# A centred pooling moved from the tensor engine to the vector engine, and one panel computed channel by channel, in a two-block transformer kernel

## The reference, cut to what matters

```python
POOL_GROUPS, POOL_GROUP_DIM = 4, 512
POOL_WINDOWS = (2, 4, 8, 16)

def centred_multiscale_pool(u):
    """u (B, L, G, Cg): group g averages over a centred window POOL_WINDOWS[g]
    (valid positions only), via prefix sums, minus the token itself."""
    ...
    left = win // 2
    right = win - 1 - left
    hi = jnp.minimum(t + right + 1, L)
    lo = jnp.maximum(t - left, 0)
    s = cs[:, hi, g] - cs[:, lo, g]
    mean = s / (hi - lo)
    return mean - uf

def pool_branch(h, w_in, w_grp, b_grp, scale, w_out):
    u, gate = jnp.split(h @ w_in, 2, axis=-1)
    p = centred_multiscale_pool(u.reshape(B, L, POOL_GROUPS, POOL_GROUP_DIM))
    p = jnp.einsum('blgc,gcd->blgd', p, w_grp) + b_grp
    y = p.reshape(B, L, POOL_WIDTH) * scale
    return (y * jax.nn.silu(gate)) @ w_out

# around it, for the latent and for the context sequence:
shift, scale, gate = jnp.split(jax.nn.silu(c) @ ada_w[i] + ada_b[i], 3, axis=-1)
h = rms_norm(x, pre_norm[i]) * (1 + scale) + shift
x = x + gate * rms_norm(pool_branch(h, ...), post_norm[i])
```

## Time and profile before

| | before |
|---|---|
| median of 3 runs | 2297.24 us |
| profiled execution: time | 2297.67 us |
| profiled execution: span, first to last instruction | 2295.9 us |
| mean granted clock of the tensor engine | 0.998 |
| tensor engine busy | 2269.0 us (99%) |
| vector engine busy | 1678.0 us (73%) |
| ScalarE busy | 1028.4 us (45%) |
| moved by DMA | 430.33 MB |

### The profile page before, as it was taken

The page is one execution under the profiler, slowest core; times in us unless marked ns, Lnnn a source line. Parts: engine busy times, 40 slices in busy tenths (PEclk is TensorE's granted clock), DMA queues, the critical chain, the costliest instruction groups (busy, mean ns, idle before and its releaser), DMA issues.

```text
span 2295.9 us, 30903 instructions
## 1 busy us (share of the span) xinstructions
PE 2269.0 (99%) x11041; PEld 1885.9 (82%) x11041; DVE 1678.0 (73%) x2399; ACT 1028.4 (45%) x1474; POOL 81.5 (4%) x115
## 2 busy tenths in 40 slices
PE   8999999999999999999999999999999999999998
PEld 6878888888888888788888888888888799999986
DVE  5479976688788887666659676766785788788864
ACT  5575655565555555443452222222322544543433
POOL 1023200000000000000000000000000100000000
PEclk9999999999999999999999999999999999999999
DMA  8966645676777676676746555555565367633344
GB/s 244 218 179 209 189 146 165 189 239 210 220 220 232 215 229 219 227 242 214 233 146 203 171 174 160 174 171 167 208 200 158 105 189 222 186 107 112 112 147 147
DMA packets 226233, 430.33 MB, mean 187 GB/s; under 512 B 13879, under 2 KB 38703, under 8 KB 225232
## 3 DMA queue, kind: packets, MB, share of 16 engines
q1 hardware_dynamic: 222400, 418.96, 58.9%
q10 hardware_dynamic: 3152, 9.83, 1.3%
q0 software_dynamic: 576, 0.14, 0.0%
HBM read 426.16 MB, written 2.72 MB: 187 GB/s over the span
## 4 chain that ended last, share of the span: by engine, by line
PE 90%; DVE 3%; DMA 2%; issue 2%; ACT 2%; DVEq 0%; SPq 0%; POOL 0%; ACTq 0%; POOLq 0%
PE ps L644 53%; PE ps L679 13%; PE ps L656 10%; PE ps L2661 2%; PE ps L2636 2%; PE ps L2697 1%; DMA raw<-in_w_up 1%; DVE lo L582 1%; PE ps L2675 1%; PE ps L2526 1%; DVE ustage L1838 1%; PE ps L693 1%; PE ps L2423 1%; PE ps L2689 1%; ACT ustage L1399 1%
## 5 line engine op out<-in xcount | busy, mean ns | idle before, releaser
L578 ACT ACTIVATE hi<-raw 128x1024 fp32r<-128x1024 f32 x604 | 634.4, 1060 | 921.6 <-PE ps L644 424.9
L582 DVE TENSOR_TENSOR lo<-raw,hi 128x1024 fp32r<-128x1024 f32 x604 | 730.9, 1223 | 414.4 <-ACT hi L578 411.7
L613 DVE SCALAR_TENSOR_TENSOR ada_acc<-raw,csil,ada_acc 128x512 f32<-128x512 f32 x660 | 452.3, 750 | 6.6 <-DMA raw<-in_ada_w 6.6
L644 PE MATMUL ps<-hi,h_hi 128*128 128x512 f32 x960 | 382.1, 398 | 0.5 <-DVE lo L582 0.2
L644 PE MATMUL ps<-hi,h_lo 128*128 128x512 f32 x960 | 378.8, 395 | 0.0
L644 PE MATMUL ps<-lo,h_hi 128*128 128x512 f32 x960 | 378.7, 395 | 0.0
L644 PE MATMUL ps<-hi,g 128*128 128x512 f32 x704 | 224.9, 398 | 2.4 <-DVE lo L582 2.4
L644 PEld LDWEIGHTS ps<-hi,h_hi 128*128 128x128 f32 x960 | 180.8, 188 | 44.3 <-DVE lo L582 3.7
L644 PEld LDWEIGHTS ps<-hi,h_lo 128*128 128x128 f32 x960 | 180.8, 188 | 42.4
L644 PEld LDWEIGHTS ps<-lo,h_hi 128*128 128x128 f32 x960 | 180.9, 188 | 40.6
L644 PEld LDWEIGHTS ps<-hi,g 128*128 128x128 f32 x704 | 133.3, 189 | 33.5 <-DVE lo L582 2.9
(11 more groups left out here) (334 smaller groups left out, 3469.8 us busy)
## 6 DMA issues: line engine op xcount, KB each, us to landing
raw<-in_ada_w SPq DMA_DIRECT2D x176, 512.0 KB, 4.2
raw<-in_w_up SPq DMA_DIRECT2D x176, 512.0 KB, 4.5
raw<-in_w_down SPq DMA_DIRECT2D x88, 512.0 KB, 4.8
raw<-in_w_in SPq DMA_DIRECT2D x84, 512.0 KB, 4.6
raw<-in_pool_w_in SPq DMA_DIRECT2D x64, 512.0 KB, 4.5
raw<-in_mla_w_in SPq DMA_DIRECT2D x56, 448.0 KB, 3.9
raw<-in_w_out SPq DMA_DIRECT2D x32, 512.0 KB, 3.7
raw<-in_pool_w_out SPq DMA_DIRECT2D x32, 512.0 KB, 4.4
```

The lines of the kernel that those rows point to most:

```text
L578: act.activation(hi[:, to, :, :], raw[:, slot, :, :], ACT.Copy).then_inc(hi_split, 1 + ada)
L582: dve.tensor_tensor(lo[:, to, :, :], raw[:, slot, :, :], hi[:, to, :, :].bitcast(F32), ALU.subtract).then_inc(lo_split, 1)
L613: ins = dve.scalar_tensor_tensor(acc, raw[:, slot, k, :], csil[:, v, kt:kt + 1], acc, ALU.mult, ALU.add)
L644: mm = pe.matmul(ps[:, bank, 0:n], tokens(a, kt0 + k, tok), w[:, slot, k, col0:col0 + n], start=first and k == 0 and s == 0, stop=last and ...
```

## The change

1. `u` is made channel by channel (`by_channels` in place of `by_tokens`), so it comes out as channels by tokens, the form in which it is needed. The halves of the first panel become matmuls of 256 columns, twice as many.
2. ACT copies it, in two halves of two channel tiles, into `upad`, which has zeros on both sides of each sequence (set once by GpSimd).
3. The pooling matrix and its 32 matmuls a group go. The vector engine sums shifted rows instead: window 2 is one addition, 4, 8 and 16 are two, three and four, each on the sum before it, for either half. One small multiplication corrects the ends of the sequences (`edges`), and one instruction scales the sum and subtracts the token (`scalar_tensor_tensor`, in place in `upad`). These stand amid the splitting of w10 to w13.
4. The group's own matrix moves from w12 and w13 to w14 and w15. The instruction that adds bias and scale moves from DVE to ACT; the bias is multiplied by the scale once, ahead of the stage.
5. The banks change: `u` in banks 0, 1, 6, 7 for group 0 and 0 to 3 for the others, the gate in 2 to 5 and then 4 to 7. The group's second modulation panel, which was turned before w17, is turned in the next group's first panel, between w1 and w2, into two of the gate's banks. For this the tensor engine waits on `gate_silu4` at the start of a group (two of the four silus of the group before) and again before that turn.
6. The panel before w16 (the first of the group) is turned before w17 now.

```diff
+        def window_sums(e, n, half):
+            step = sums_done(n, half) - n - 2
+            spans = [(0, SEQ)]
+            for level in range(n, 0, -1):
+                spans.insert(0, (spans[0][0] - 2 ** (level - 1), spans[0][1] + 2 ** (level - 1)))
+            src = upad[:, 2 * half:2 * half + 2, :, :].rearrange("p m s t -> p (m s) t")
+            buffers = windows[half][0], windows_first2[n] if half == 0 else windows[1][1]
+            for level, (a, b) in enumerate(spans):
+                to = buffers[level % 2]
+                back, ahead = (1, 0) if level == 0 else (2 ** (level - 1), 2 ** (level - 1))
+                if level:
+                    e.wait_ge(window_summed, step + level)
+                e.tensor_tensor(to[:, :, reach + a:reach + b], src[:, :, reach + a - back:reach + b - back],
+                                src[:, :, reach + a + ahead:reach + b + ahead], ALU.add).then_inc(window_summed, 1)
+                src = to
+                yield
+            left = POOL_WINDOWS[n] // 2
+            ends = src[:, :, reach:reach + SEQ].rearrange("p r (a l) -> p r a l", l=left)[:, :, 0:SEQ // left:SEQ // left - 1, :]
+            e.wait_ge(window_summed, step + n + 1)
+            e.tensor_tensor(ends, ends, edges[:, n, :, 0:left].unsqueeze(1).to_broadcast([P, 4, 2, left]), ALU.mult).then_inc(window_summed, 1)
+            yield
...
         (vector engine, pool_group)
-                split(place_of(0) + RING, place_of(CH + 2) + RING)
+                split(place_of(0) + RING, place_of(4) + RING)
+                if n:
+                    take_ada(dve, ada0 - 1, GATE_BANKS[n][0])
+                split(place_of(4) + RING, place_of(CH) + RING)
+                dve.wait_ge(u_ready, 2 * n + 2)
+                dve.wait_ge(edges_loaded, 17)
+                sums = itertools.chain(window_sums(dve, n, 0), window_sums(dve, n, 1))
+                for k in range(3):
+                    for _ in itertools.islice(sums, -(-2 * (n + 2) // 3)):
+                        pass
+                    split(place_of(CH + k) + RING, place_of(CH + k + 1) + RING)
+                for half in range(2):
+                    dve.wait_ge(window_summed, sums_done(n, half))
+                    v = upad[:, 2 * half:2 * half + 2, :, reach:reach + SEQ].rearrange("p m s t -> p (m s) t")
+                    dve.scalar_tensor_tensor(v, window_total(n, half)[:, :, reach:reach + SEQ], 1.0 / POOL_WINDOWS[n], v,
+                                             ALU.mult, ALU.subtract).then_inc(pooled, 1)
+                    if half == 0:
+                        split(place_of(CH + 3) + RING, place_of(CH + 4) + RING)
...
-                split(place_of(CH + 2) + RING, place_of(CH + 6) + RING)
-                dve.wait_ge(chunks_used, i * step + used(C_POOL + place_of(CH + 5) + 1))
-                for m in range(4):
-                    ch = n * 4 + m
-                    ins = dve.tensor_scalar(y[:, bass.ds(ch, 1), :].rearrange("p a b -> p (a b)"), ps[:, m, :],
-                                            cols[:, bass.ds(ch + V_POOL_B[0] * P + V_POOL_B[1], 1)],
-                                            cols[:, bass.ds(ch + V_POOL_S[0] * P + V_POOL_S[1], 1)], ALU.add, ALU.mult)
-                ins.then_inc(grouped, 1)
-                split(place_of(CH + 6) + RING, place_of(CH + 8) + RING)
+                split(place_of(CH + 4) + RING, place_of(CH + 8) + RING)
...
         (ScalarE, pool_group)
-                act.activation(u[:, :, :], ps[:, 0:4, :], ACT.Copy).then_inc(u_ready, 1)
+                for half in (1, 0):
+                    b0 = U_BANKS[n][2 * half]
+                    act.activation(upad[:, 2 * half:2 * half + 2, :, reach:reach + SEQ],
+                                   ps[:, b0:b0 + 2, :].rearrange("p m (s t) -> p m s t", s=2), ACT.Copy).then_inc(u_ready, 1)
...
+                his(act, C_POOL, i, step, ahead(CH + 4), ahead(CH + 8))
+                act.wait_ge(chunks_used, done(CH + 7))
+                for m in range(4):
+                    ins = act.activation(y[:, n * 4 + m, :], ps[:, U_BANKS[n][m], :], ACT.Identity,
+                                         scale=col(V_POOL_S, n * 4 + m), bias=col(V_POOL_B, n * 4 + m))
+                ins.then_inc(grouped, 1)
...
         (tensor engine, pool_group)
-                    pe.wait_ge(ada_taken, FREE + ada0)
-                    panel_by_tokens(pe, C_POOL, i, POOL_ORDER, e * POOL_W, h4_hi, h4_lo, streams, W)
+                    pe.wait_ge(ada_taken, FREE + ada0 - 1)
+                    pe.wait_ge(gate_silu4, (n - 1) * 4 + 2)
+                    for j in range(CH):
+                        if j == 2:
+                            pe.wait_ge(gate_silu4, n * 4)
+                            last = C_POOL + POOL_ORDER.index((True, (2 * ((n - 1) % 2) + 2) * CH - 1))
+                            pe.wait_ge(lo_split, (n - 1) // 2 * step + last + RING + 1)
+                            turn_ada(pe, ada0 - 1, 1, GATE_BANKS[n][0])
+                        at = C_POOL + place(POOL_ORDER, e * POOL_W + j)
+                        by_channels(pe, i * step + at, split_slot(at), h4_hi, h4_lo, CK_T * j, U_BANKS[n], j == 0, j == CH - 1, ada_behind(at))
...
-                for m in range(4):
-                    for s in range(2):
-                        for k in range(TT):
-                            mm = pe.matmul(ps[:, m, s * SEQ + c0:(s + 1) * SEQ], u[:, TT * (1 - s) + k, m * P:(m + 1) * P],
-                                           poolm[:, bass.ds(n, 1), k, c0:].rearrange("p a b -> p (a b)"),
-                                           start=k == 0, stop=k == TT - 1)
-                    mm.then_inc(pooled, 1)
```

More of the change, by code:

```diff
@@ L648, in by_tokens, with by_channels @@
             return mm
-        def by_channels(pe, c, slot, a_hi, a_lo, kt0, bank0, first, last, ada=0):
+        def by_channels(pe, c, slot, a_hi, a_lo, kt0, banks, first, last, ada=0, part=slice(0, NT * P), frees=True):
             pe.wait_ge(lo_split, c + RING + 1)
@@ L1037, in two_block_kernel, with sums_done, window_total @@
         GATE0 = Q_RANK + KV_RANK + ROPE
+        def window_sums(e, n, half):
[19 more added lines that the diff above has]
+            yield
+        def sums_done(n, half):
+            return 2 * sum(m + 2 for m in range(n)) + (half + 1) * (n + 2)
+        def window_total(n, half):
+            return (windows[half][0], windows_first2[n] if half == 0 else windows[1][1])[n % 2]
         VECS = vectors(t)
@@ L2530, in pool_group @@
-                for j in range(2, 4):
-                    chunk(j, h4_hi, h4_lo, CK_T * j, 4, False, False)
+                pe.wait_ge(ada_taken, FREE + ada0)
+                for j in range(6):
+                    chunk(j, h4_hi, h4_lo, CK_T * j, GATE_BANKS[n], j == 0, False)
+                pe.wait_ge(u_ready, 2 * n + 2)
                 pe.wait_ge(pt_lo_done, FREE + n + 1)
-                for j in range(4, 6):
-                    chunk(j, pt_hi, pt_lo, CK_T * (j - 4), 0, j == 4, j == 5)
@@ L2535, in pool_group @@
-                for j in range(6, 10):
-                    if j == 8:
+                for j in range(6, 8):
+                    chunk(j, pt_hi, pt_lo, CK_T * (j - 6), U_BANKS[n], j == 6, j == 7)
+                for j in range(8, 10):
+                    if j == 9:
                         pe.wait_ge(grouped, FREE + n + 1)
-                        pe.wait_ge(lo_split, i * step + C_POOL + POOL_ORDER.index((True, (2 * e + 1) * CH - 1)) + RING + 1)
+                        pe.wait_ge(lo_split, i * step + C_POOL + POOL_ORDER.index((True, (2 * e + 1 + n // (POOL_G - 1)) * CH - 1)) + RING + 1)
```

125 lines of the change are left out of this document (66 added, 59 removed).

## The result

| | before | after |
|---|---|---|
| median | 2298.15 us (8 runs) | 2306.27 us (8 runs, 2303.36 to 2310.7) |
| ratio after / before | | 1.0038, 95% interval 1.0029 to 1.0046 |
| profiled execution: time | 2297.67 us | 2303.36 us |
| profiled execution: span | 2295.9 us | 2301.6 us |
| mean granted clock of the tensor engine | 0.998 | 0.995 |

The change makes the kernel 8 to 9 us slower (6.7 to 10.6 by the interval). The forecast was 2296.9 us with a range up to 2303. The profiled execution is the quickest of its eight runs; 5.7 us of the difference can be followed in it.

The account below looks back on a forecast made before the run. The prediction took the tensor engine to bound the pooling stage; -21.2 + 0.3 + 7.3 + 8.6 + 4.7 = -0.3 us gave 2296.9 us against the median, with an 8-in-10 range of 2288 to 2303 us.

Parts of the forecast that it names:

- What bounds the kernel: Pooling stage: tensor engine busy 449.78 of 450 us, so each matmul removed saves its time unless another engine comes late.
- what goes: Tensor engine, pooling stage: the removed pooling matmuls save 5.31 us in each of four groups, -21.2 us.
- the halves: First panel on the tensor engine: 96 matmuls of 512 columns become 192 of 256, +0.3 us.
- The eight transposes: Tensor engine, each modulation panel: its eight transposes stay and only change place, costing nothing.
- The wait at a group's start: Tensor engine, w0 of groups 1 to 3: waits for two silus, 2.43 us three times, +7.3 us.
- The vector engine between u and w14: Window sums make it late for w11 and w14: groups 1 to 3 late by 0.2, 2.8, 5.6 us, +8.6.
- the upper bound: Window sums of groups 1 to 3 at the stage's dearest rate per element: +9.1 us more than the forecast.
- the rival with dear sums: Window sums ahead of w11 and w14, groups 1 to 3, cost more than the addition's row: 2306.0 us, chance 0.14.
- The dependence between sums: Vector engine: each window sum waits for the one before, starting 0.04 us after its end.
- The clock: Tensor engine's clock falls behind two idle times above 2.42 us and half of three near 2.2: 3.5 x 1.35, +4.7 us.

Follow-up runs that it names:

- e5_all: Changed kernel with second turn's wait relaxed, group-start silu waits removed or moved behind 12 matmuls, w10's splitting and two modulation chunks ahead of the sums: 2279.72 us, ratio 0.992.
- e1_turn: Changed kernel, but in the last group the second modulation panel is turned without waiting for the first one's taking: 2301.23 us, ratio 1.0011.
- e6_inter: Changed kernel with the two halves' window sums taken in turn, so none directly follows the one it depends on: 2303.45 us, ratio 1.0019.
- e4_fill: Changed kernel with unread matmuls added ahead of w0 in groups 1 to 3 and of w14 in groups 2 and 3: 2300.42 us, ratio 1.0003.
- e3_early: Changed kernel with w10's hi ahead of the copies of u, and w10's lo, a8 and a9 ahead of the window sums: 2296.56 us, ratio 0.9989.
- e7_nopool: Kernel before the change with most of each group's pooling matmuls left out, 4 of 16 remaining: 2282.41 us, ratio 0.993 to that kernel.

## Why the prediction was wrong, point by point

- **What bounds the kernel; what goes; the halves**: right. -20.9 forecast, -20.74 measured (e5_all), and 5.31 a group against 5.32.
- **The eight transposes "stay, only elsewhere: nothing"**: this is the step that failed. The transposes themselves cost nothing more than before. But point 6 of the change puts the first panel's turn ahead of w17, so in the last group it stands directly before the second one, and the second waits on `ada_taken`. I priced the instructions of a moved turn and not the wait inside `turn_ada`, nor what stands ahead of the release on the vector engine: four `y_low`, which wait for ScalarE's `y_high`, and these had moved 13.3 us later (1596.90 to 1610.22) behind a `hi` that waits for w16. Its price was 4.8 us and the fall behind it, 6.2 us by e1_turn. With it the sum of the forecast would have been about +6, 2303 us, just at the range's end; the clock term below is the other part of the miss.
- **The wait at a group's start**: the mechanism is right, and nearly the size (2.43 forecast, 2.63 measured, three times). ScalarE's part came as read from the earlier trace rows; its timeline in the changed kernel:

```profile
1290.02 1.07 ACT L1552 ACTIVATE gsilu<-ps 128x512 f32<-128x512 f32 x2
```

  The second silu ends at 1291.09, and the matmul starts at 1291.34, 0.25 later. The 0.05 of the earlier trace rows is the vector engine's, not ScalarE's.
- **The vector engine between u and w14**: right in its places, somewhat high in size: 8.6 against 7.7. Group 1 was not late, group 2 by 2.4 (2.8), group 3 by 1.6 and 3.4 (2.0 and 3.6). The sums' durations were those of the addition in the earlier trace rows, and the upper bound, the rival with dear sums, is out. That rival's time (2306.0) is the measured one, but its cause is not: it got there by another way.
- **The dependence between sums**: 0.04 beyond the end forecast from the earlier trace rows, 0.04 measured (1554.16 + 1.28, then 1555.48), and e6_inter shows what independent ones do: 1.20 apart. The Trainium skill (VectorE: DVE Perf Modes, section The DRAIN you can't avoid) says that a semaphore after each instruction costs nothing extra; these runs show something else for a sum that waits for the one before it, which costs 0.12 us more (1.32 against 1.20).
- **The clock**: too low in number and in size. A fall costs 1.55 and more, not 1.35: the one of the earlier trace rows, from which I took the size, is a little shorter than those here. And I let half of the idle times near 2.4 fall. In all profiled executions of the changed kernel and its variants, the tensor engine's idle times within the stage, by the length shown:

| idle time, us | 0.3 to 1.8 | 2.17 to 2.23 | 2.38 | 3.2 to 4.5 |
|---|---|---|---|---|
| clock fell | 0 of 11 | 2 of 4 | 10 of 12 | 8 of 8 |

  So the three at the groups' starts mostly fell. They are 2.38 long in every profiled execution that has them, and their outcome varies from one to the next; what decides it, no run here shows.
In short: of the 9.4 us between the forecast and the median, 4.8 are the missed wait, and 0.9 is that the kernel before itself came out at 2298.15 rather than 2297.24. The smaller errors nearly cancel, and some 4 us are left. The profiled execution has 1.6 of them as clock falls (6.3 against 4.7, the missed wait's own among them). That the rest is falls too is an estimate: by the table above an average run has about five, four of them at the places that e4_fill fills, where the profiled one has four in all, and the one behind the turn can cost up to 2.9.

## What to carry to other kernels

When a step is moved, follow its wait to the releasing engine and read what stands ahead of the release there in the written order, before and after; two calls of a helper that were a chunk apart and become neighbours can wait for each other. When work that needs a new result is put into an engine's order, first look at how long the engine will stand still for that result, and move work that doesn't need it ahead: that alone was worth 11 us here by the runs, 9 by the rows (e3_early). A wait for a bank should name the one bank that is shared and stand directly before its first use; other banks' matmuls go first.

## What the runs showed of the hardware

- A plain float32 matmul of 256 or 136 columns is recorded as two instructions; counting records counts each twice (32 records, 16 matmuls; 8 records for 4 in e7_nopool).
- A vector addition that waits for the one before it starts 1.32 us behind that one's start (1554.16 to 1555.48), an independent one of the same width 1.20 (e6_inter).
- An idle time of 2.38 us, the same in each profiled execution, left the clock up in two of twelve cases; behind the other ten it fell. Forty-two added matmuls, whose result nobody reads, made the changed kernel 8 us faster (uncertain by some 3) by filling such idle times (e4_fill).
